# The mixer's products ordered term by term over the heads, with row and column halves of the TensorE array taking turns

## What is computed

```python
def step(s, inp):
    r_t, w_t, k_t, v_t, kk_t, b_t = inp
    sa = jnp.einsum('dbhvk,dbhk->dbhv', s, -kk_t)
    s = s * w_t[..., None, :] + sa[..., None] * b_t[..., None, :] + v_t[..., None] * k_t[..., None, :]
    return s, jnp.einsum('dbhvk,dbhk->dbhv', s, r_t)
...
o = gla_chunked(q, k, v, g_f) + flip(gla_chunked(flip(q), flip(k), flip(v), flip(g_b)))
```

## Time and profile before

| | us |
|---|---|
| median of 3 runs | 3757.97 |
| lowest and highest | 3755.13, 3760.62 |
| the profiled execution | 3761.1 |
| its span | 3759.3 |
| busy: TensorE matmuls | 3392.0 (90%) |
| busy: TensorE weight loads | 2378.9 (63%) |
| busy: VectorE | 1307.9 (35%) |
| busy: ScalarE | 818.9 (22%) |
| busy: GpSimd | 142.8 (4%) |

### The profile page before, as it was taken

The page is one execution under the profiler, slowest core; times in us unless marked ns, Lnnn a source line. Parts: engine busy times, 40 slices in busy tenths (PEclk is TensorE's granted clock), DMA queues, the critical chain, the costliest instruction groups (busy, mean ns, idle before and its releaser), DMA issues.

```text
span 3759.3 us, 41294 instructions
## 1 busy us (share of the span) xinstructions
PE 3392.0 (90%) x17145; PEld 2378.9 (63%) x17145; DVE 1307.9 (35%) x1862; ACT 818.9 (22%) x1262; POOL 142.8 (4%) x200
## 2 busy tenths in 40 slices
PE   7899968999998899979878997999889997969898
PEld 6686755444443688845643444888668875648798
DVE  1433242000002444445252112444444445251265
ACT  1211111111112322221241002222232222140243
POOL 0021101110110000000000000000000000000000
PEclk9898868999999899989978999999999999989999
DMA  5635344999999122211100211222122221203352
GB/s 228 246 136 202 113 189 180 421 421 421 421 421 387 67 90 101 90 45 66 35 1 34 78 67 69 100 90 100 67 79 101 89 92 67 77 1 134 127 188 79
DMA packets 77485, 556.30 MB, mean 148 GB/s; under 512 B 8480, under 2 KB 9504, under 8 KB 10384
## 3 DMA queue, kind: packets, MB, share of 16 engines
q1 hardware_dynamic: 76208, 548.44, 37.7%
q0 software_dynamic: 1120, 5.57, 0.4%
HBM read 552.93 MB, written 1.05 MB: 147 GB/s over the span
## 4 chain that ended last, share of the span: by engine, by line
PE 80%; DVE 10%; DMA 7%; ACT 2%; issue 1%; POOL 0%; DVEq 0%; SPq 0%; POOLq 0%; ACTq 0%
PE bank L544 60%; PE bank L831 9%; DMA ring<-slabs 7%; PE bank L554 1%; PE bank L1100 1%; PE bank L671 1%; DVE tiny L1945 1%; PE bank L682 1%; PE bank L1119 1%; PE bank L679 1%; ACT ht L1231 1%; PE bank L586 1%; DVE xt L1893 1%; DVE rs L1535 1%; DVE wk L1982 1%
## 5 line engine op out<-in xcount | busy, mean ns | idle before, releaser
L544 PE MATMUL bank<-ht,ring 128*128 128x256 f32 (+1 forms) x1760 | 548.2, 469 | 43.0 <-DVE wk L1983 19.8
L544 PE MATMUL bank<-hhi,whi 128*128 128x512 f32 (+1 forms) x1408 | 518.3, 368 | 61.1 <-DVE hlo L1882 61.1
L544 PE MATMUL bank<-hlo,whi 128*128 128x512 f32 (+1 forms) x1408 | 515.9, 366 | 0.0
L544 PE MATMUL bank<-hhi,wlo 128*128 128x512 f32 (+1 forms) x1408 | 510.4, 363 | 0.0
L544 PEld LDWEIGHTS bank<-ht,ring 128*128 128x128 f32 x1760 | 341.6, 194 | 231.4 <-issue 154.9
L831 PE MATMUL bank<-ring,wk 128*64 128x512 f32 x1872 | 429.4, 600 | 15.5 <-DMA ring<-slabs 14.8
L544 PE MATMUL bank<-fhl,whi 128*128 128x512 f32 (+1 forms) x1408 | 399.8, 371 | 11.9 <-DVE wlo L1521 11.9
L1521 DVE TENSOR_TENSOR wlo<-ring,whi 128x2048 fp32r<-128x2048 f32 x132 | 298.3, 2287 | 303.8 <-ACT whi L1208 303.7
L544 PEld LDWEIGHTS bank<-hhi,whi 128*128 128x128 f32 x1408 | 266.6, 189 | 110.3 <-DVE hlo L1882 64.0
L1208 ACT ACTIVATE whi<-ring 128x2048 fp32r<-128x2048 f32 x132 | 251.3, 1908 | 325.6 <-PE bank L544 325.6
L544 PEld LDWEIGHTS bank<-hhi,wlo 128*128 128x128 f32 x1408 | 267.1, 190 | 45.4
(11 more groups left out here) (340 smaller groups left out, 3301.7 us busy)
## 6 DMA issues: line engine op xcount, KB each, us to landing
ring<-slabs SPq DMA_DIRECT2D x522, 1024.0 KB, 9.5
wk<-mixp POOLq DMA_DIRECT2D x1, 1040.0 KB, 12.6
xt<-xT SPq DMA_DIRECT2D x1, 1024.0 KB, 6.2
xt<-ctxT POOLq DMA_DIRECT2D x1, 1024.0 KB, 12.4
out<-xt POOLq DMA_DIRECT2D x1, 1024.0 KB, 5.0
cst<-maskc POOLq DMA_DIRECT2D x1, 960.0 KB, 14.4
cst<-attc POOLq DMA_DIRECT2D x1, 896.0 KB, 16.0
keep<-keepc POOLq DMA_DIRECT2D x1, 320.0 KB, 8.2
```

Of the source, the lines that this page charges most:

```text
L544: last = pe.matmul(o, a, b, start=k == 0, stop=k == len(pairs) - 1)
```

## The change

Four places are written in another order; the same products are computed.

1. Head products: for each pair of heads, BT of the even head, BT of the odd head, then KH of the even and of the odd one, so that the two row halves of the array take turns. The wait for the odd head's bank now stands ahead of the even head's KH product.
2. w1 and the output: the loop over the terms is the outer one, the heads are the inner one. Only the first matmul of a bank (and partition half) has the start flag, and the last ones have the stop flag.
3. State: the same, and the term with VT comes ahead of the one with SA.
4. GLA scores and output: the two row halves take turns, and the output goes term by term; both `go` signals now come at the very end.

```diff
@@ -646,17 +646,16 @@
                     u = 2 * d + step
                     tt = ts if step == 0 else 1 - ts
                     tok = slice(tt * P, (tt + 1) * P)
-                    for h in range(8):
-                        n = 8 * u + h
-                        j, lo = h // 2, 64 * (h % 2)
-                        hi = lo + 64
-                        b = 2 + h % 4
-                        if h >= 4:
-                            pe.wait_ge(sem("matc"), n - 3)
+                    for j in range(4):
                         for k, src in enumerate((BT, KH)):
-                            mm = pe.matmul(bank[b][:, k * 256:(k + 1) * 256], src[lo:hi, j, tok],
-                                           KR[lo:hi, j, tt, :, :], start=True, stop=True)
-                        mm.then_inc(sem("mat"), 1)
+                            for par in range(2):
+                                h, lo = 2 * j + par, 64 * par
+                                if h >= 4 and k == 0:
+                                    pe.wait_ge(sem("matc"), 8 * u + h - 3)
+                                mm = pe.matmul(bank[2 + h % 4][:, k * 256:(k + 1) * 256], src[lo:lo + 64, j, tok],
+                                               KR[lo:lo + 64, j, tt, :, :], start=True, stop=True)
+                                if k:
+                                    mm.then_inc(sem("mat"), 1)
                     ada(ADA_MAT)
                     pe.wait_ge(sem("matc"), 8 * u + 8)
                     if step == 0:
@@ -689,13 +688,14 @@
 
                     if step:
                         pe.wait_ge(sem("stc"), d + 1)
-                    for h in range(8):
-                        j, lo = h // 2, 64 * (h % 2)
-                        terms = [(MT[:, h, 256:384], VT[:, tt, h * HD:(h + 1) * HD])]
-                        if step:
-                            terms.append((KR[lo:lo + 64, j, tt, 0, :], ST[lo:lo + 64, j, :]))
-
-                        group(bank[2 * (h % 2)][:, j * HD:(j + 1) * HD], terms, "w1" if h == 7 else None)
+                    for term in range(1 + step):
+                        for h in range(8):
+                            j, lo = h // 2, 64 * (h % 2)
+                            a, v = ((MT[:, h, 256:384], VT[:, tt, h * HD:(h + 1) * HD]) if term == 0 else
+                                    (KR[lo:lo + 64, j, tt, 0, :], ST[lo:lo + 64, j, :]))
+                            mm = pe.matmul(bank[2 * (h % 2)][:, j * HD:(j + 1) * HD], a, v,
+                                           start=term == 0 and h < 2, stop=term == step and h >= 6)
+                    mm.then_inc(sem("w1"), 1)
                     pe.wait_ge(sem("w1c"), u + 1)
 
                     for h in range(8):
@@ -705,20 +705,24 @@
                     pe.wait_ge(sem("sac"), u + 1)
 
                     if step == 0:
+                        for term in range(2):
+                            for h in range(8):
+                                j, lo = h // 2, 64 * (h % 2)
+                                hs = slice(h * HD, (h + 1) * HD)
+                                a, v = ((KHK[:, hs], VT[:, tt, hs]), (BTK[:, hs], SA[:, hs]))[term]
+                                mm = pe.matmul(bank[4][lo:lo + 64, j * HD:(j + 1) * HD], a, v,
+                                               start=term == 0 and h < 2, stop=term == 1 and h >= 6)
+                        mm.then_inc(sem("stp"), 1)
+
+                    for term in range(2 + step):
                         for h in range(8):
                             j, lo = h // 2, 64 * (h % 2)
                             hs = slice(h * HD, (h + 1) * HD)
-                            group(bank[4][lo:lo + 64, j * HD:(j + 1) * HD],
-                                  [(BTK[:, hs], SA[:, hs]), (KHK[:, hs], VT[:, tt, hs])],
-                                  "stp" if h == 7 else None)
-
-                    for h in range(8):
-                        j, lo = h // 2, 64 * (h % 2)
-                        hs = slice(h * HD, (h + 1) * HD)
-                        terms = [(VT[:, tt, hs], MT[:, h, 384:512]), (SA[:, hs], MT[:, h, P:256])]
-                        if step:
-                            terms.append((ST[lo:lo + 64, j, :], KR[lo:lo + 64, j, tt, 1, :]))
-                        group(bank[5][lo:lo + 64, j * P:(j + 1) * P], terms, "yb" if h == 7 else None)
+                            a, v = ((VT[:, tt, hs], MT[:, h, 384:512]), (SA[:, hs], MT[:, h, P:256]),
+                                    (ST[lo:lo + 64, j, :], KR[lo:lo + 64, j, tt, 1, :]))[term]
+                            mm = pe.matmul(bank[5][lo:lo + 64, j * P:(j + 1) * P], a, v,
+                                           start=term == 0 and h < 2, stop=term == 1 + step and h >= 6)
+                    mm.then_inc(sem("yb"), 1)
                     if step == 0:
                         pe.wait_ge(sem("ybc"), u + 1)
 
@@ -741,14 +745,15 @@
             mm.then_inc(sem("gtr"), 1)
             pe.wait_ge(sem("gtrc"), 1)
             for d in range(2):
-                for par in range(2):
-                    lo = 64 * par
-                    for tt in range(2):
-                        for j in range(2):
+                for tt in range(2):
+                    for j in range(2):
+                        for par in range(2):
+                            lo = 64 * par
                             tok = slice(tt * P, (tt + 1) * P)
                             mm = pe.matmul(b3(2 * d + par, 4)[:, 2 * tt + j, :], KG[lo:lo + 64, 2 * d + j, tok],
                                            QH[lo:lo + 64, 2 * d + j, tok], start=True, stop=True)
-                    mm.then_inc(sem("gmat"), 1)
+                            if tt == j == 1:
+                                mm.then_inc(sem("gmat"), 1)
             pe.wait_ge(sem("gtrc"), 2)
             for d in range(2):
                 for h in range(4):
@@ -759,17 +764,20 @@
             ada(ADA_GMAT)
             pe.wait_ge(sem("gmatc"), 4)
             pe.wait_ge(sem("gstc"), 1)
-            for par in range(2):
+            for term in range(3):
                 for tt in range(2):
                     d = 1 - tt
                     for j in range(2):
-                        lo, h = 64 * par, 2 * j + par
-                        tok = slice(tt * P, (tt + 1) * P)
-                        vh = VG[:, tt, h * P:(h + 1) * P]
-                        group(b3(par, 4)[:, 2 * tt + j, :],
-                              [(vh, DT[:, 0, tt, h, :]), (vh, DT[:, 1, tt, h, :]),
-                               (STG[lo:lo + 64, d, j, :], QH[lo:lo + 64, 2 * d + j, tok])],
-                              "go" if tt == j == 1 else None)
+                        for par in range(2):
+                            lo, h = 64 * par, 2 * j + par
+                            tok = slice(tt * P, (tt + 1) * P)
+                            vh = VG[:, tt, h * P:(h + 1) * P]
+                            a, v = ((vh, DT[:, 0, tt, h, :]), (vh, DT[:, 1, tt, h, :]),
+                                    (STG[lo:lo + 64, d, j, :], QH[lo:lo + 64, 2 * d + j, tok]))[term]
+                            mm = pe.matmul(b3(par, 4)[:, 2 * tt + j, :], a, v, start=term == tt == j == 0,
+                                           stop=term == 2 and tt == j == 1)
+                            if term == 2 and tt == j == 1:
+                                mm.then_inc(sem("go"), 1)
 
 
             pe.wait_ge(sem("goc"), 2)
```

## The result

| | before | changed |
|---|---|---|
| median of the runs taken side by side | 3756.55 us (3751.95 to 3760.62) | 3718.22 us (3715.48 to 3722.5) |
| ratio, 95% interval | | 0.9899 (0.9882 to 0.9916) |
| profiled execution, its span | 3761.1, 3759.3 us | 3718.05, 3716.2 us |
| PE busy, PEld busy | 3392.0, 2378.9 us | 3344.5, 2349.5 us |
| output projection to end | 3211.8 us | 3209.6 us |

The change is faster by 38.3 us, 1.0%. The forecast was 3716, 2.2 us under the median. A second measurement stands among the experiments: 3720.13.

What follows compares the result with a forecast made beforehand. TensorE was taken to bound the mixer's chain, except at the head products (VectorE's masks). Savings of 16.3 + 15.0 (two directions) + 10.7 (GLA) = 42.0 us take the profiled 3761.1 to 3719.1, median 3716; range 3708 to 3734.

Steps and rivals of the forecast that it cites:

- w1, 2.8 a direction: Step 1 of each mixer direction: w1 takes 3.0 us in place of 5.83; 1.8 saved at the high bound.
- sa, 1.7: Untouched sa products behind w1 in step 1: full clock gives 2.0 us in place of 3.69; lower end 0.
- Output of step 1, 10.0: Scan output, each direction: 3.3 us at full clock in place of 13.36; 7.0 saved at half clock.
- Lines 633 and 728, 1.8 and 0.5: Untouched products behind the two directions' outputs, 7.17 and 2.05 us: half of the full-clock gain of 3.6 and 1.0.
- State terms, 0: State products of the scan: nothing saved, since step 0 already has pairs.
- Head products, 0: Head products, four times: TensorE could drop from 4.83 to about 3.7 us, but VectorE's 4.89 us of masks end last.
- GLA scores 1.3, output 8.2, copies -0.66, norm sum 1.9: GLA part: scores 5.06 to 3.7 us, output 13.05 to 4.9, ScalarE's copies lose cover, norm sum 3.80 to 1.9.
- 5 us more: Best bounds of lines 633, 728 and 781 over the forecast; with run scatter of 3 they set the lower end, 3708.
- Low clock throughout: Rival: clock stays low in the same mixer and GLA stretches; 24 us saved, 3734 us; chance 0.20.
- No overlap: Rival: array halves don't overlap, only changes of shape go; output 5.7 us, 33 us saved, 3725 us; chance 0.09.
- A drain at each turn: Rival: each turn between halves drains the array, 0.2 us, nothing overlaps; about 30 us slower, 3788 us; chance 0.02.
- The gain doesn't reach the end: Rival: experts behind the mixer are bound by their slabs' stream, which starts no earlier; no change, 3758 us; chance 0.03.

Runs made afterwards that it cites:

- The part alone: One hunk in the kernel before: under w1, only w1 term by term, 3746.91 us; under head products, only head products in turns, 3756.7 us.
- the part without w1: Only the scan's state and output term by term, in the kernel before, w1 left old: 3730.41 us, ratio 0.9943.
- the filled kernel: Changed kernel with three modulation slabs per step moved from the levels into the waits around sa and behind the output: 3710.81 us.
- the old w1 with filling: Kernel before, old order of products, with modulation slabs moved into the waits as in the filled kernel: 3739.46 us.
- the four kernels with one part each: Kernel before with only head products, w1, state and output, or GLA changed: 3756.7, 3746.91, 3730.41, 3747.04 us.
- the run without filling: Changed kernel with even heads first, then odd, in w1, state and output, so no turns between halves: 3722.94 us.

## Why the forecast held, step by step

- **w1, 2.8 a direction: right.** 5.83 to 2.99, twice. The part alone gives it too. Row halves in turns take 1.11 for 16 records, against 1.0 taken and 1.95 as the high bound. Without turns 1.60.
- **sa, 1.7: right**, 2.01 and 2.15 for 3.69, and for the reason given: the part with w1 alone has it at 2.01, the part without w1 at 3.69.
- **Output of step 1, 10.0: right about the mechanism, mis-sized.** It saved 8.98 and 7.77. The step that failed is the sentence "3.3 us at full clock" as the case of this kernel: I gave the clock to the output because it was given to w1 and sa. In fact it falls to 0.50 behind sa and its two waits, and in the first direction comes back within the output, about 2.6 us after its start. At full clock (the filled kernel) it is 2.92 us, so the working of the 3.3 was 0.4 too high.
- **Lines 633 and 728, 1.8 and 0.5: low.** 3.5 and 0.85 came, nearly all that the bounds allowed. They paid back 2.0 of the 3.3 us that the outputs lacked.
- **State terms, 0: not quite.** They and the output of step 0 took 4.54 us in both directions, against 4.53 and 2.96 before. The 1.6 us lost is the clock's fall behind sa, which the old order of these terms shows in six of its eight unfilled step 0s and the new one in six of eight as well, so it is not a price of the new order. The prediction looked at the second direction's step 0 alone.
- **Head products, 0: right**, with the part alone at 1.0002. Head 4's product behind the wait for head 1's mask left no gap in the masks (4.87 us).
- **GLA scores 1.3, output 8.2, copies -0.66, norm sum 1.9: right against that execution**: 1.34, 8.26, -0.5, 1.79. But the 13.05 us they start from is one draw. In four of five executions the old order has the full clock there and 8.35 us, and then the GLA part gives about 4 us, not 11. A sum from one profile could not see this; it is the likely reason that the medians differ by 38.3 where the profiles differ by 43.1, likely only, since before and changed were each profiled too few times to count how often the clock is low there.
- **How much of the hit is luck.** The mechanism was right for w1, sa and the order of the output. That the total came within 2.2 us is luck in part: the saving of the GLA part was some 6 us too high for the execution that came in four of five, that of the outputs 3.3 too high, that of lines 633 and 728 2.0 too low. Also, the 42.0 were taken from a median of 3758; from the 3756.55 measured beside the changed kernel they would give 3714.5, 3.7 under the result. And the "5 us more" under the range's lower end add to 4.2 from the three lines that it names; nothing hangs on it.
- **Not foreseen: the late release of slabs.** The prediction said that "removing ten of its 14 idle microseconds takes no slab away". It counted DMA traffic and not the signals that `group` sends beside its matmuls. No price of it could be measured.

**The rivals.** Low clock throughout is refuted, though it is true of one place: there is a fall behind sa, in each step 1 over within the output, and in both step 0s as well (clock 0.63). Against this rival the prediction held that step 0 of the second direction keeps 1.00 with the same gaps; step 0 of the first direction, in the same trace, did not (0.66). Its thought that the gate follows busy time, which the Trainium skill, "TensorE: Matmul & The Clock Gate", has in its section on what's actually happening, is at odds with the rows if it is taken as their busy time: the clock was 0.50 at 13.35 of 14.00 us busy and at 3.00 of 3.00 in the old w1 with filling, and 1.00 at 3.92 of 4.00 in the new w1 and at 2.00 of 2.10 in sa behind it. The busy share of the rows does not tell these apart. Nor does the mixture of shapes alone: it had 0.50 in the old w1 with filling, but 1.00 in the old GLA output in four of five executions, and the fall behind sa in step 0 comes without it. The runs show that regrouping took the low clock out of w1 and sa, and that filling the waits took it out of what follows; what sets the clock they leave open. "No overlap" asked for an output of 5.7 at clock 1.00; it was 2.92 there. The weight-load rule that the Trainium skill has on the same page, in its section on packing small matmuls (loads overlap only where the row groups differ), would make the 32 column-half records 3.4 us, by the prediction's estimate; the filled kernel has 1.97 again, in step 1. A drain at each turn, 0.2 us, is refuted by w1's 1.11 us with seven turns in it. "The gain doesn't reach the end" is refuted by the tail: from the output projection to the end 3211.8 before, 3209.6 after, and 3209.2 to 3211.1 in the four kernels with one part each.

## What to carry to other kernels

Matmuls that use a part of the array should stand in runs of one shape, with the halves in turns: with the waits filled alike the order of the products was worth 29 us here. The turns between halves are 3 to 5 of them, by the run without filling. The rest is that a mixture of shapes pays for each change, and that the clock was low in the old w1 and in sa behind it. Where a stretch has PEclk 0.50, read the timeline by shape and look at what stands ahead of it, since busy time doesn't show it; dense work that has to be done anyway belongs into the waits there, or into a wait that nothing else fills. Before a helper is replaced, list every signal that it sends, and before a sum is made from a stretch at half clock, look at that stretch in a second execution.

## What was not expected of the hardware

- TensorE can be busy 3.00 of 3.00 us and be granted 0.50, in the midst of a mixture of 128-row and 64-row shapes that began at full clock.
- The same instructions in the same place had clock 0.50 in one execution and 1.00 in four others: 13.05 against 8.35 us.
- A granted clock that had fallen came back while column halves ran in turns (0.50 in 285 to 288, 0.96 in 288 to 290.6).
- Behind the same two short waits around sa the clock fell in most executions of step 0 and stayed up in some (4.53 and 2.96 us in one trace); with slabs in the waits it stayed up in all six.
- Row halves in runs instead of in turns took 1.60 us for 16 records, between 1.11 in turns and the 1.95 of one after another. Why isn't settled.
